# Latent attention's probabilities: transposed by VectorE in 32 by 32 blocks instead of by TensorE

## The chip, the cores and the metric

One core of one Trainium2 chip. The metric is the device time of one execution in microseconds (us). The kernel before has a median of 2431.6 us over 3 runs (2429.13 to 2432.31).

## The reference

Two layers of a hybrid transformer run over one sequence of 256 tokens, width 2048, all in float32. Layer 0 mixes gated linear attention (8 heads) with latent attention (8 heads, 128 columns each plus 64 rotary columns), layer 1 is sparse attention with a compressed, a selected and a window branch; each layer has a gated FFN (5632) and a gated input of 256 columns per token. The part that matters here is the latent attention of layer 0:

```python
q_rope = apply_rope(q[..., MLA_NOPE:], cos64[:, None], sin64[:, None])
k_rope = apply_rope(k_r, cos64, sin64)[:, None]
...
o_mla = causal_attention_blocks(qm, km, kv[..., MLA_NOPE:], (MLA_NOPE + MLA_ROPE) ** -0.5)
...
s = jnp.einsum('bhqd,bhkd->bhqk', qb, k).astype(jnp.float32) * scale
s = jnp.where(kpos[None, :] <= qpos[:, None], s, NEG)
p = jax.nn.softmax(s, axis=-1)
return jnp.einsum('bhqk,bhkd->bhqd', p.astype(v.dtype), v)
```

With 256 tokens and blocks of 128, one head has three 128 by 128 tiles of probabilities: queries 0 to 127 against keys 0 to 127, and queries 128 to 255 against both halves of the keys. The product with the values needs each tile with the keys on the partitions, that is transposed.

## The kernel before, in words

**Weights.** Every weight matrix is streamed from HBM in "units" of 128 partitions by 4 chunks by 512 columns into `raw` (4 buffers, SP's queue, `unit` at L385). To keep float32 accuracy with fp32r products, ScalarE rounds a unit to `wh` (L1048, `split`), VectorE forms the rest `wl = raw - wh` (L1472, `split`), and TensorE multiplies (activations high by `wh`, activations low by `wh`, activations high by `wl`: 24 matmuls of 512 columns, L546). `whl` has two buffers, so ScalarE can round unit n only when the products of unit n-2 are done. TensorE asks for `hi_ready` at a unit's start and for `lo_ready` ahead of its last third.

**Slots and gaps.** Units are grouped in slots; slot s, unit j is written (s, j). Other work is put by hand in the gaps behind units. TensorE does the work of gap (s, j) right behind the products of unit (s, j) (`gap`, L784). ScalarE and VectorE do theirs (`at_gap`, L1187 and L1817) behind the `split` of a later unit, by the tables `STAGED_ACT` and `STAGED_DVE` (L138): two units later in the slots of this change. Each engine works strictly in the order of its program.

**Latent attention** sits in the gaps of slots KG, VG and VG+1 (11, 12, 13; the code writes them as UKV+2 to UKV+4). It takes two heads at a time: `MLA_AT` (L78) puts step t at gaps (11,1), (11,3), (12,1), (12,3), (13,1), (13,3) for t = 0 to 5. On TensorE `mla_step(t)` (L603) first waits for `att_v`, VectorE's word that its stage t-1 is over. Then, for t from 2, it multiplies the values with the transposed probabilities of step t-2 (12 matmuls, L614) from `PT0` into `MB`; for t from 1 to 4 it transposes the six 128 by 128 tiles of step t-1 (L620) from `SP0` through `MB`; for t below 4 it forms the scores of step t (L627 and L633) and signals `s_done`. On VectorE `mla_stage(t)` (L1592) is `softmax` (L1568: scaling and mask from `MB` to `SP0`, two maxima, a wait for ScalarE's exponentials at L1094, a reciprocal, four scalings in place) and, for t from 2, the low part of the output (L1599). Its last instruction signals `att_v`. On ScalarE `mla_stage(t)` (L1097) copies the transposed tiles from `MB` to `PT0` (L1100, one instruction of 128 by 768, signals `pt_sb`), does the exponentials, and rounds the output (L1106). `SP0` and `PT0` have one buffer each. `pt_sb` and `pt_done` are also counted on by the sparse attention of layer 1, behind the 4 steps of latent attention.

The FFN already transposes its hidden activations in another way: `quadrant` (L2029) issues four `V.transpose` instructions (L2036), each on 32 partitions by 256 elements, that transpose 32 by 32 blocks and put them in the right quadrant of partitions of `HT`.

Of the kernel before, what the change touches and what calls it, by code (L numbers as in the profile page):

```python
# [12 lines left out]
ACT = mybir.ActivationFunctionType  # L13
AX = mybir.AxisListType

P = 128
# [10 lines left out]
MLA_SCALE = float((128 + 64) ** -0.5)  # L27
# [48 lines left out]
MLA_STEPS = 4  # L76
NSA_STEPS = 16
MLA_AT = {(UKV + 2, 1): 0, (UKV + 2, 3): 1, (UKV + 3, 1): 2, (UKV + 3, 3): 3, (UKV + 4, 1): 4, (UKV + 4, 3): 5}  # L78


def nsa_plan():
# [114 lines left out]
def build(nc, T):  # L196
# [15 lines left out]
    with ctx:  # L212
# [9 lines left out]
        def sem(name):  # L222
            return ctx.enter_context(nc.semaphore(name))
# [11 lines left out]
        ident = sb("ident", [P, P])  # L235
# [30 lines left out]
        def zt(name, off, shape, dt=F32):  # L266
            assert off + int(np.prod(shape[1:])) * 4 <= ZS, name
            return nc.alloc_sbuf_tensor_at(name, shape, dt, offset=z0 + off)
# [5 lines left out]

        qg, kg = zt("qg", 0, [P, NT, 512]), zt("kg", 4096, [P, NT, 512])
        vg, gg = zt("vg", 8192, [P, NT, 1024]), zt("gg", 16384, [P, NT, 1024])
        SP0, PT0 = zt("SP0", 16384, [P, 2, 384]), zt("PT0", 19456, [P, 2, 384])
        QnT, KnT = zt("QnT", 24576, [P, 8, SEQ]), zt("KnT", 32768, [P, 8, SEQ])
        Vm, zc = zt("Vm", 40960, [P, NT, 1024]), zt("zc", 40960, [P, NT, 1104])
        qr, QrT = zt("qr", 49792, [P, NT, 512]), zt("QrT", 53888, [P, 4, SEQ])  # L280
# [55 lines left out]
        s_done, pt_done, pv_done = sem("s_done"), sem("pt_done"), sem("pv_done")  # L336
        s_read = sem("s_read")
        mx_ok, exp_ok, o_hi = sem("mx_ok"), sem("exp_ok"), sem("o_hi")
        pt_sb = sem("pt_sb")
        att_v, p_ok, head_ok = sem("att_v"), sem("p_ok"), sem("head_ok")  # L340

        ga_ps, ga_t, ga_n, ga_l, ga_ok = (sem(n) for n in ("ga_ps", "ga_t", "ga_n", "ga_l", "ga_ok"))
# [172 lines left out]
        def _(pe):  # L515
# [87 lines left out]
            def mla_step(t):  # L603
                if t:
                    pe.wait_ge(att_v, t)
                if t > 1:
                    pe.wait_ge(pt_sb, min(t - 1, MLA_STEPS))
                if 2 <= t:
                    for b in range(2):
                        hd = 2 * (t - 2) + b  # L610
                        for m in range(NT):
                            for kt in range(m + 1):
                                p0 = (m + kt) * P
                                last = mm(MB[:, 2 * b + m, 384:512], Vm[:, kt, hd * P:(hd + 1) * P],  # L614
                                          PT0[:, b, p0:p0 + P], start=(kt == 0), stop=(kt == m))
                    last.then_inc(pv_done, 1)
                if 1 <= t <= MLA_STEPS:
                    for b in range(2):
                        for k in range(3):
                            last = nc.tensor.transpose(MB[:, 2 + b, k * P:(k + 1) * P],  # L620
                                                       SP0[:, b, k * P:(k + 1) * P], ident[:, :])
                    last.then_inc(pt_done, 1)
                if t < MLA_STEPS:
                    for b in range(2):
                        hd = 2 * t + b
                        for m in range(NT):
                            mm(MB[:, b, m * P:m * P + (m + 1) * P], QnT[:, hd, m * P:(m + 1) * P],  # L627
                               KnT[:, hd, 0:(m + 1) * P], start=(m == 0), stop=False, skip_group_check=True)

                    for m in range(NT):  # L630
                        for b in range(2):
                            r = slice(64 * b, 64 * b + 64)
                            last = mm(MB[:, b, m * P:m * P + (m + 1) * P], QrT[r, t, m * P:(m + 1) * P],  # L633
                                      KrT[r, 0:(m + 1) * P], start=False, stop=True, skip_group_check=True)
                    last.then_inc(s_done, 1)
# [4 lines left out]
            def nsa_step(t):  # L640
                if t == 0:
                    pe.wait_ge(kt_sb, 4)
                if 2 <= t:
                    g, j = (t - 2) // 4, (t - 2) % 4
                    pe.wait_ge(pt_sb, MLA_STEPS + t - 1)
                    pe.wait_ge(pct_sb, g + 1)
                    mm(MB[:, 2, 0:SEQ], VB[:, g, j, :], PcT[:, g % 2, :], start=True, stop=False)  # L647
                    for b, v in enumerate((vs, vw)):
                        mm(MB[:, 2, 0:SEQ], v[:, 0, g * P:(g + 1) * P], PT1[:, b, 0:SEQ], start=False, stop=False)  # L649
                    for b, v in enumerate((vs, vw)):  # L650
                        last = mm(MB[:, 2, P:SEQ], v[:, 1, g * P:(g + 1) * P], PT1[:, b, SEQ:3 * P],  # L651
                                  start=False, stop=b == 1)
                    last.then_inc(pv_done, 1)
                if t in CP_STEP:
                    pe.wait_ge(cs_ok, CP_STEP[t] + 1)
                    for m in range(NT):
                        last = nc.tensor.transpose(MB[:, 3, m * P:(m + 1) * P],
                                                   Pc[:, m, :, :].rearrange("p j n -> p (j n)"), ident[:, :])
                    last.then_inc(cp_ps, 1)
                if t < NSA_STEPS:  # L660
                    g, j = t // 4, t % 4
                    if t:
                        pe.wait_ge(mx_ok, MLA_STEPS + t)
                    else:
                        pe.wait_ge(c2_v, 1)
                        pe.wait_ge(c2_a, 1)
                    for b in range(2):
                        for m in range(NT):
                            last = mm(MB[:, b, m * P:m * P + (m + 1) * P], QT[:, g % 2, j, m * P:(m + 1) * P],  # L669
                                      (ksT, kwT)[b][:, g, 0:(m + 1) * P], start=True, stop=True)  # L670
                    last.then_inc(s_done, 1)
                if 1 <= t <= NSA_STEPS:
                    pe.wait_ge(p_ok, t)
                    if t > 1:
                        pe.wait_ge(head_ok, t - 1)
                    pe.wait_ge(pct_sb, sum(c <= t for c in CP_STEP))
                    for b in range(2):
                        for k in range(3):
                            last = nc.tensor.transpose(MB[:, 2 + b, k * P:(k + 1) * P],  # L679
                                                       SP1[(t - 1) % 2][:, b, k * P:(k + 1) * P], ident[:, :])  # L680
                    last.then_inc(pt_done, 1)
# [351 lines left out]
        def _(act):  # L1033
# [61 lines left out]
                last.then_inc(exp_ok, 1)  # L1095

            def mla_stage(t):  # L1097
                if 1 <= t <= MLA_STEPS:
                    act.wait_ge(pt_done, t)
                    A(PT0[:, :, :], MB[:, 2:4, 0:384], ACT.Copy).then_inc(pt_sb, 1)  # L1100
                if t < MLA_STEPS:
                    exps(t, SP0)
                if t >= 2:
                    act.wait_ge(pv_done, t - 1)
                    for b in range(2):
                        last = A(XBh[:, 2 * (t - 2) + b, :].rearrange("p (m t) -> p m t", m=2),  # L1106
                                 MB[:, 2 * b:2 * b + 2, 384:512], ACT.Copy)
                    last.then_inc(o_hi, 1)

            def nsa_stage(t):  # L1110
                if t >= 2:
                    act.wait_ge(pv_done, MLA_STEPS + t - 1)
                    A(XMID[1][0][:, t - 2, :], MB[:, 2, 0:SEQ], ACT.Copy).then_inc(o_hi, 1)  # L1113
                if t in CP_STEP:
                    g = CP_STEP[t]
                    act.wait_ge(cp_ps, g + 1)
                    A(PcT[:, g % 2, :], MB[:, 3, 0:SEQ], ACT.Copy).then_inc(pct_sb, 1)
                if t < NSA_STEPS:
                    exps(MLA_STEPS + t, SP1[t % 2])
                if 1 <= t <= NSA_STEPS:  # L1120
                    act.wait_ge(pt_done, MLA_STEPS + t)
                    A(PT1[:, :, :], MB[:, 2:4, 0:384], ACT.Copy).then_inc(pt_sb, 1)

            def gla_stage(k):
# [333 lines left out]
        def _(v):  # L1458
# [109 lines left out]
            def softmax(t, SP, scale, gate=None, meanwhile=lambda: None):  # L1568
# [20 lines left out]
                        last = V.tensor_scalar(c, c, sm[:, k:k + 1], None, ALU.mult)  # L1589
                return last  # L1590

            def mla_stage(t):  # L1592
                if t < MLA_STEPS:
                    last = softmax(t, SP0, MLA_SCALE)
                if t >= 2:
                    v.wait_ge(o_hi, t - 1)
                    for b in range(2):
                        x = [q[:, 2 * (t - 2) + b, :].rearrange("p (m t) -> p m t", m=2) for q in XB]
                        last = V.tensor_tensor(x[1], MB[:, 2 * b:2 * b + 2, 384:512], x[0].bitcast(F32), ALU.subtract)  # L1599
                last.then_inc(att_v, 1)  # L1600
# [216 lines left out]
            def at_gap(k):  # L1817
# [2 lines left out]
                    split_in(XB, 4, TQ["cqkv"], 0, 64)  # L1820
                if k in MLA_AT:
                    mla_stage(MLA_AT[k])
                if k in GLA_AT:
                    gla_stage(GLA_AT[k])
                if k == (OUT0, 2):
# [382 lines left out]
```

## Time and profile before

| | |
|---|---|
| median of 3 runs | 2431.6 us |
| profiled execution, own time | 2429.38 us |
| its span in the trace | 2427.7 us |
| granted TensorE clock, mean | 0.999 |
| latent attention's steps on TensorE | from 145 us to 217 us of the span |

The span is the time from the first to the last instruction on the core; the execution's own time is 1.7 us longer. In the views, PE is TensorE's matmuls, PEld its weight loads, DVE VectorE, ACT ScalarE, SP the queue that issues the weights' transfers. A row of the timeline gives the start, the time from there to the end of the last instruction of the row, the engine, the source line, what is written and read, the count, and in brackets the idle time ahead of it on its engine with what ended it.

### The profile page before, as it was taken

What the parts mean: (1) busy time and instruction counts of PE and PEld (TensorE: products, weight loads), DVE (VectorE), ACT (ScalarE), POOL (GpSimd) and SP (SyncE); (2) the same over time, 40 slices, a digit from 0 to 9 for tenths busy, and PEclk for the clock granted to TensorE, in tenths of its full rate; (3) what the DMA queues carried; (4) which work ended last, traced back from release to release, by engine and by line L of the source; (5) the groups of instructions that cost most, each with busy time, mean ns of one, the idle gap of its engine ahead of it and who ended that gap; (6) DMA issues with size and microseconds to landing.
All of it is one profiled execution on the core that took longest, in us unless ns stands there. A gap on an engine that the chain in (4) does not pass through costs nothing.

```text
span 2427.7 us, 29112 instructions
## 1 busy us (share of the span) xinstructions
PE 2398.8 (99%) x11640; PEld 2003.2 (83%) x11640; DVE 1499.5 (62%) x1572; ACT 1047.4 (43%) x1003; POOL 20.5 (1%) x38
## 2 busy tenths in 40 slices
PE   7999999999999999999999999999999999999999
PEld 7887888888888888888888888888888888888887
DVE  4654756666466655667676677566664667446675
ACT  5444445343333433345544355463343434334443
POOL 0000100000000000000000000000000000000000
PEclk9999999999999999999999999999999999999999
DMA  7554456665556556556555633465556665565564
GB/s 227 189 173 125 174 175 211 195 195 194 191 191 191 194 197 196 174 181 219 190 191 179 209 120 107 144 208 191 191 193 196 197 192 190 191 193 193 176 218 138
DMA packets 226967, 449.04 MB, mean 185 GB/s; under 512 B 7961, under 2 KB 19233, under 8 KB 225586
## 3 DMA queue, kind: packets, MB, share of 16 engines
q1 hardware_dynamic: 225218, 440.72, 55.5%
q10 hardware_dynamic: 1648, 6.89, 0.8%
q8 instruction: 74, 1.21, 0.2%
q14 instruction: 27, 0.22, 0.0%
HBM read 445.48 MB, written 2.10 MB: 184 GB/s over the span
## 4 chain that ended last, share of the span: by engine, by line
PE 97%; DVE 2%; ACT 1%; issue 0%; DMA 0%; ACTq 0%; DVEq 0%
PE PG L546 89%; PE MB L546 1%; PE MB L877 1%; PE MB L669 1%; PE MB L649 1%; PE MB L679 0%; ACT whl L1048 0%; DVE whl L1472 0%; PE MB L647 0%; PE MB L651 0%; PE MB L688 0%; PE PG L590 0%; PE PG L591 0%; PE PG L592 0%; PE MB L614 0%
## 5 line engine op out<-in xcount | busy, mean ns | idle before, releaser
L1472 DVE TENSOR_TENSOR whl<-raw,whl 128x2048 fp32r<-128x2048 f32 (+4 forms) x435 | 955.8, 2198 | 762.5 <-ACT whl L1048 762.2
L1048 ACT ACTIVATE whl<-raw 128x2048 fp32r<-128x2048 f32 (+4 forms) x435 | 800.8, 1841 | 1167.0 <-PE PG L546 1151.1
L546 PE MATMUL PG<-whl,XBh 128*128 128x512 f32 (+1 forms) x3376 | 796.6, 386 | 0.9 <-DVE whl L1472 0.5
L546 PE MATMUL PG<-whl,XAh 128*128 128x512 f32 (+1 forms) x3136 | 741.9, 387 | 2.2 <-ACT whl L1048 2.2
L546 PEld LDWEIGHTS PG<-whl,XBh 128*128 128x128 f32 x3376 | 624.9, 188 | 127.5 <-DVE whl L1472 0.9
L546 PEld LDWEIGHTS PG<-whl,XAh 128*128 128x128 f32 x3136 | 584.1, 188 | 119.1 <-ACT whl L1048 3.0
L546 PE MATMUL PG<-whl,XBl 128*128 128x512 f32 (+1 forms) x1688 | 412.5, 386 | 0.0
L546 PE MATMUL PG<-whl,XAl 128*128 128x512 f32 (+1 forms) x1568 | 383.4, 386 | 0.0
L546 PEld LDWEIGHTS PG<-whl,XBl 128*128 128x128 f32 x1688 | 313.1, 188 | 63.2
L546 PEld LDWEIGHTS PG<-whl,XAl 128*128 128x128 f32 x1568 | 291.9, 188 | 57.1
L2036 DVE STREAM_TRANSPOSE HT<-Hb 32x256 f32<-32x256 f32 x352 | 153.4, 436 | 5.6
L1989 DVE TENSOR_TENSOR Hb<-Eb,PG 128x1024 f32<-128x1024 f32 x22 | 26.8, 1216 | 8.8 <-PE PG L546 8.8
L1337 ACT ACTIVATE Eb<-PG,rsh 128x512 f32<-128x512 f32 x44 | 27.5, 675 | 5.4 <-DVE rsq L1522 5.4
L1606 DVE TENSOR_TENSOR XAl<-MB,XAh 128x256 fp32r<-128x256 f32 x16 | 6.8, 423 | 36.3 <-ACT XAh L1113 36.3
L1982 DVE SCALAR_TENSOR_TENSOR Eb<-Eb,PG 128x1024 f32<-128x1024 f32 x22 | 26.7, 1215 | 3.0 <-ACT Eb L1337 3.0
L877 PE MATMUL MB<-ident,h 128*128 128x128 f32 x192 | 26.5, 281 | 0.4 <-ACT posT L1262 0.4
L877 PEld LDWEIGHTS MB<-ident,h 128*128 128x128 f32 x192 | 23.3, 145 | 3.9 <-ACT posT L1262 0.6
L1094 ACT ACTIVATE SP1a<-SP1a,sm 128x128 f32<-128x128 f32 (+1 forms) x32 | 14.2, 445 | 25.0 <-DVE sm L1578 25.0
L503 POOL TENSOR_TENSOR pwo<-pwi,mhalf 128x2 f32<-128x2 f32 (+2 forms) x6 | 8.7, 1445 | 1875.6 <-DVE pwi L1532 1817.2
L1543 DVE SCALAR_TENSOR_TENSOR h<-Fm,pwo,h 128x512 f32<-128x512 f32 (+1 forms) x40 | 23.2, 639 | 0.1
L1094 ACT ACTIVATE SP1b<-SP1b,sm 128x128 f32<-128x128 f32 (+1 forms) x32 | 14.2, 446 | 21.0 <-DVE sm L1578 21.0
L1487 DVE SCALAR_TENSOR_TENSOR XAl<-MB,vcol,XAh 128x256 fp32r<-128x256 f32 x32 | 13.2, 476 | 14.2 <-ACT XAh L1060 14.2
(341 smaller groups left out, 1007.0 us busy)
## 6 DMA issues: line engine op xcount, KB each, us to landing
raw<-in_ffn_w_gate SPq DMA_DIRECT2D x88, 1024.0 KB, 5.2
raw<-in_ffn_w_up SPq DMA_DIRECT2D x88, 1024.0 KB, 5.2
raw<-in_ffn_w_down SPq DMA_DIRECT2D x64, 1024.0 KB, 5.0
raw<-in_nsa_w_in SPq DMA_DIRECT2D x36, 1024.0 KB, 5.1
raw<-in_ple_w_gate SPq DMA_DIRECT2D x32, 1024.0 KB, 5.1
raw<-in_ab_w_in SPq DMA_DIRECT2D x24, 1024.0 KB, 5.3
raw<-in_ffn_w_down SPq DMA_DIRECT2D x32, 768.0 KB, 4.3
raw<-in_ab_w_out SPq DMA_DIRECT2D x16, 1024.0 KB, 5.3
```

The lines of the kernel that those rows point to most:

```text
L546: return mm(bank(m), X[x][:, chunk, m * P:(m + 1) * P], w[:, k, c * ncol:(c + 1) * ncol], start=x == 0 and w is wh and c == 0 and pos in ( ...
L649: mm(MB[:, 2, 0:SEQ], v[:, 0, g * P:(g + 1) * P], PT1[:, b, 0:SEQ], start=False, stop=False)
L669: last = mm(MB[:, b, m * P:m * P + (m + 1) * P], QT[:, g % 2, j, m * P:(m + 1) * P], (ksT, kwT)[b][:, g, 0:(m + 1) * P], start=True, stop= ...
L877: t = nc.tensor.transpose(MB[:, b % 4, o:o + P], h[:, m, k:k + P], ident[:, :])
L1048: A(wh[:, place % 2, 0:w], raw[:, place, 0:w], ACT.Copy).then_inc(hi_ready, 1)
L1094: last = A(c, c, ACT.Exp, bias=sm[:, k:k + 1], accum_out=sm[:, 4 + k:5 + k])
L1337: last = A(Eb[:, m, :], PG[:, b % 2, m, :], ACT.Tanh, scale=rsh[:, 1 + 2 * layer, m:m + 1])
L1472: V.tensor_tensor(wl[:, k, 0:w], raw[:, place, 0:w], wh[:, k, 0:w].bitcast(F32), ALU.subtract).then_inc(lo_ready, 1)
L1543: V.scalar_tensor_tensor(h[:, m, c], Fm[:, m, c], pwo[:, m:m + 1], h[:, m, c], ALU.mult, ALU.add).then_inc(upd, 1)
L1982: V.scalar_tensor_tensor(Eb[:, :, :], Eb[:, :, :], 1.0, PG[:, b % 2, :, :], ALU.add, ALU.mult).then_inc(evac_v, 1)
L1989: V.tensor_tensor(Hb[:, :, :], Eb[:, :, :], PG[:, (b + 1) % 2, :, :], ALU.mult).then_inc(evac_v, 1)
L2036: last = V.transpose(dst[:, :, :, a, :], src[:, :, :, q, :])
```

## The change: what it does

Six transposes on TensorE and the copy on ScalarE are gone from each of the four steps. In their place VectorE issues 16 `V.transpose` instructions for each step, of 32 partitions by 192 elements (2 heads, 3 tiles, 32 columns), from `SP0` to `PT0`. Eight of them (query rows 0 to 63) stand in `mla_stage(t)` behind the softmax, ahead of the signal `att_v`; the other eight (rows 64 to 127) stand in the gap one unit on (`MLT_AT`: (11,2), (12,0), (12,2), (13,0)) and end in the new signal `pt_v`. `PT0` has two buffers, by t % 2; the second lies at byte 50816 of the shared region, behind `KrT`. TensorE's products with the values wait for `pt_v` instead of `pt_sb`, and the next softmax waits for it too, as it writes over `SP0`. The counts of `pt_sb` and `pt_done` in layer 1 lose the 4 steps.

```diff
+MLT_AT = {(UKV + 2, 2): 0, (UKV + 3, 0): 1, (UKV + 3, 2): 2, (UKV + 4, 0): 3}
...
-        SP0, PT0 = zt("SP0", 16384, [P, 2, 384]), zt("PT0", 19456, [P, 2, 384])
+        SP0 = zt("SP0", 16384, [P, 2, 384])
+        PT0 = [zt("PT0a", 19456, [P, 2, 384]), zt("PT0b", 50816, [P, 2, 384])]
...
-        pt_sb = sem("pt_sb")
+        pt_sb, pt_v = sem("pt_sb"), sem("pt_v")
...
             def mla_step(t):
                 if t:
                     pe.wait_ge(att_v, t)
-                if t > 1:
-                    pe.wait_ge(pt_sb, min(t - 1, MLA_STEPS))
                 if 2 <= t:
+                    pe.wait_ge(pt_v, t - 1)
                     for b in range(2):
                         hd = 2 * (t - 2) + b
                         for m in range(NT):
                             for kt in range(m + 1):
                                 p0 = (m + kt) * P
                                 last = mm(MB[:, 2 * b + m, 384:512], Vm[:, kt, hd * P:(hd + 1) * P],
-                                          PT0[:, b, p0:p0 + P], start=(kt == 0), stop=(kt == m))
+                                          PT0[t % 2][:, b, p0:p0 + P], start=(kt == 0), stop=(kt == m))
                     last.then_inc(pv_done, 1)
-                if 1 <= t <= MLA_STEPS:
-                    for b in range(2):
-                        for k in range(3):
-                            last = nc.tensor.transpose(MB[:, 2 + b, k * P:(k + 1) * P],
-                                                       SP0[:, b, k * P:(k + 1) * P], ident[:, :])
-                    last.then_inc(pt_done, 1)
...
             def mla_stage(t):
-                if 1 <= t <= MLA_STEPS:
-                    act.wait_ge(pt_done, t)
-                    A(PT0[:, :, :], MB[:, 2:4, 0:384], ACT.Copy).then_inc(pt_sb, 1)
...
+            def blocks(t, rows):
+                for a in rows:
+                    src = SP0[32 * a:32 * a + 32, :, :].rearrange("p b (k q i) -> p b k q i", k=3, q=4)
+                    for q in range(4):
+                        dst = PT0[t % 2][32 * q:32 * q + 32, :, :].rearrange("p b (k a j) -> p b k a j", k=3, a=4)
+                        last = V.transpose(dst[:, :, :, a, :], src[:, :, :, q, :])
+                return last
+
             def mla_stage(t):   
                 if t < MLA_STEPS:
-                    last = softmax(t, SP0, MLA_SCALE)
+                    if t:
+                        v.wait_ge(pt_v, t)
+                    step(softmax(t, SP0, MLA_SCALE))
+                    last = blocks(t, (0, 1))
                 if t >= 2:
                     v.wait_ge(o_hi, t - 1)
...
                 if k in MLA_AT:
                     mla_stage(MLA_AT[k])
+                if k in MLT_AT:
+                    blocks(MLT_AT[k], (2, 3)).then_inc(pt_v, 1)
```

## Rows read from the trace of the kernel before

**Rows 1.** The page: busy time by engine, and the chain that ended last.

```profile
PE 2398.8 (99%) x11640; PEld 2003.2 (83%) x11640; DVE 1499.5 (62%) x1572; ACT 1047.4 (43%) x1003; POOL 20.5 (1%) x38
...
PE 97%; DVE 2%; ACT 1%; issue 0%; DMA 0%; ACTq 0%; DVEq 0%
```

**Rows 2.** Timeline of PE (and one row of PEld) over latent attention: start us, us, what.

```profile
158.73 0.82 PE L620 MATMUL MB<-ident,SP 128*128 128x128 f32 x6
159.38 1.48 PE L627 MATMUL MB<-KnT,QnT 128*128 128x128 f32 x8
...
161.64 2.11 PE L546 MATMUL PG<-whl,XAh 128*128 128x512 f32 x8
...
172.43 1.21 PEld L614 LDWEIGHTS MB<-PT,Vm 128*128 128x128 f32 x9
...
172.66 1.50 PE L614 MATMUL MB<-PT,Vm 128*128 128x128 f32 x12
174.00 0.82 PE L620 MATMUL MB<-ident,SP 128*128 128x128 f32 x6
...
203.17 1.50 PE L614 MATMUL MB<-PT,Vm 128*128 128x128 f32 x12
204.51 0.82 PE L620 MATMUL MB<-ident,SP 128*128 128x128 f32 x6
205.08 2.08 PE L546 MATMUL PG<-whl,XAh 128*128 128x512 f32 x8
```

**Rows 3.** Timeline of DVE over the same stretch.

```profile
149.88 1.02 DVE L1573 SCALAR_TENSOR_TENSOR SP<-MB,cmask 128x384 f32<-128x384 f32 x2
...
153.87 0.18 DVE L1581 RECIPROCAL sm<-sm 128x4 f32<-128x4 f32 x1 [1.93 <-ACT SP L1094]
154.09 1.01 DVE L1589 TENSOR_SCALAR SP<-SP,sm 128x128 f32<-128x128 f32 x4
155.68 2.29 DVE L1472 TENSOR_TENSOR whl<-raw,whl 128x2048 fp32r<-128x2048 f32 x1 [0.58 <-ACT whl L1048]
160.93 2.29 DVE L1472 TENSOR_TENSOR whl<-raw,whl 128x2048 fp32r<-128x2048 f32 x1 [2.95 <-ACT whl L1048]
163.14 0.74 DVE L1527 TENSOR_SCALAR kg<-PG,rsd 128x512 f32<-128x512 f32 x1
163.80 1.01 DVE L1573 SCALAR_TENSOR_TENSOR SP<-MB,cmask 128x384 f32<-128x384 f32 x2
...
182.21 0.75 DVE L1599 TENSOR_TENSOR XBl<-MB,XBh 128x256 fp32r<-128x256 f32 x2
```

**Rows 4.** Timeline of ACT over the same stretch.

```profile
161.37 0.80 ACT L1100 ACTIVATE PT<-MB 128x768 f32<-128x768 f32 x1
...
182.73 1.92 ACT L1048 ACTIVATE whl<-raw 128x2048 fp32r<-128x2048 f32 x1 [1.15 <-PE PG L546]
```

**Rows 5.** Timeline of DVE in the FFN, where `quadrant` transposes blocks.

```profile
433.43 1.78 DVE L2036 STREAM_TRANSPOSE HT<-Hb 32x256 f32<-32x256 f32 x4
436.66 2.29 DVE L1472 TENSOR_TENSOR whl<-raw,whl 128x2048 fp32r<-128x2048 f32 x1 [1.45 <-ACT whl L1048]
438.99 1.78 DVE L2036 STREAM_TRANSPOSE HT<-Hb 32x256 f32<-32x256 f32 x4
```

**Rows 6.** Lines L2036, L1577 and L1578 on DVE: durations min/median/max in ns.

```profile
L2036 DVE STREAM_TRANSPOSE HT<-Hb x352: 425/436/444, 433.4 to 2273.5; 32x256 f32<-32x256 f32 x176
...
L1577 DVE TENSOR_REDUCE sm<-SP x4: 420/420/421, 150.9 to 194.0; 128x2 f32<-128x256 f32 x4
...
L1578 DVE TENSOR_REDUCE sm<-SP x4: 673/676/678, 151.3 to 194.4; 128x2 f32<-128x512 f32 x4
```

**Rows 7.** Timeline of PE at the start of the kernel.

```profile
15.00 2.82 PE L546 MATMUL PG<-whl,XAh 128*128 128x368 f32 x8 [2.25 <-ACT whl L1048]
...
20.10 2.84 PE L546 MATMUL PG<-whl,XAh 128*128 128x368 f32 x16
```

**Rows 8.** Stretches at the end of the kernel: us, PE busy, granted clock, DMA.

```profile
2420.00:2422.00 2.00, 1.81 (x8) 1.00 0.00 0
2422.00:2424.00 2.00, 0.00 (x0) 1.00 0.00 0
2424.00:2426.00 2.00, 0.00 (x0) 0.63 0.43 161
```

More of the change, by code:

```diff
@@ L644, in nsa_step @@
                     g, j = (t - 2) // 4, (t - 2) % 4
-                    pe.wait_ge(pt_sb, MLA_STEPS + t - 1)
+                    pe.wait_ge(pt_sb, t - 1)
                     pe.wait_ge(pct_sb, g + 1)
@@ L1120, in nsa_stage @@
                 if 1 <= t <= NSA_STEPS:
-                    act.wait_ge(pt_done, MLA_STEPS + t)
+                    act.wait_ge(pt_done, t)
                     A(PT1[:, :, :], MB[:, 2:4, 0:384], ACT.Copy).then_inc(pt_sb, 1)
```

## The prediction

> **What bounds the kernel now.** I read the page first: TensorE is busy for 99% of the span and holds 97% of the chain that ended last [rows 1]. So time is won only by taking work off TensorE, and lost whenever another engine makes it wait. VectorE is busy for 62% on average, but that average says nothing about the 60 us in which latent attention runs, so I then read the timelines of PE, DVE and ACT there.
>
> TensorE [rows 2]: step 1 runs from 158.73 to 161.64 us, 0.65 us of it the six transposes (158.73 to 159.38) and 2.26 us the scores. The two units up to the next step take 11.02 us (161.64 to 172.66). Step 2 begins with 1.34 us of products with the values (172.66 to 174.00). No row of this stretch has idle time in brackets: TensorE waits for nobody.
>
> VectorE [rows 3]: the softmax of step 0 goes from 149.88 to 155.10 us (154.09 plus 1.01), 5.22 us with the 1.93 us in which it waits for ScalarE's exponentials. Behind it comes the split of the next unit at 155.68 us. The bracket there, and the 2.95 us ahead of the next split, are VectorE's slack: two pauses, 0.58 and 2.95 us in these two units, about 3.5 us for a step.
>
> **What is removed.** Four groups of six transposes. The first takes 0.65 us, the last 0.57 us (204.51 to 205.08) [rows 2], the two between 0.66 us each (the first of them 174.00 to 174.66): 2.54 us off TensorE, 0.10% of the kernel. That is the whole possible gain. ScalarE loses four copies of 0.80 us [rows 4]. They are worth nothing: ScalarE's next split waits for TensorE anyway, by 1.15 us even in the fullest stage [rows 4], and VectorE's softmax waits for exponentials that don't come earlier.
>
> **What is added on VectorE.** 64 transposes of 32 by 192, of which the trace has no example. The nearest are those of the FFN, 32 by 256: 0.436 us each [rows 6], four from first start to last end in 1.78 us [rows 5], so (1.78 - 0.436) / 3 = 0.448 us from start to start. They don't overlap. What do 64 elements less save? Two reductions on the same engine, of 256 and 512 elements, take 0.420 and 0.676 us [rows 6]: 1.0 ns for an element. So I take 0.448 - 0.064 = 0.38 us each. The ends: 0.448 if the price doesn't depend on the length, 0.336 if it is all length (three quarters of it). I am nearer the middle because the reduction's two rows show both a fixed and a linear part. Eight transposes are 3.04 us.
>
> **Where they lie.** VectorE has 3.5 us of slack for a step and gets 2 x 3.04 = 6.1 us. So the question is what the deficit does. I walk through VectorE's order, with these pieces: a split followed by block transposes 2.33 us (436.66 to 438.99) [rows 5]; a split followed by something else 2.21 us (160.93 to 163.14) [rows 3]; the eviction of a slot, in every second stage, 0.66 us (163.14 to 163.80) [rows 3]; softmax 5.22 us; the new wait behind it 0.04 us, as the reciprocal's (153.87 plus 0.18, next start 154.09) [rows 3]; the output's low part 0.75 us from step 2 on [rows 3]. `att_v` comes behind the first eight transposes and the low part:
>
> - att_v 1: 155.10 + 0.04 + 3.04 = 158.18 us. TensorE asks for it at 158.73: just in time.
> - att_v 2: split 2.33, eight transposes 3.04, split 2.21, eviction 0.66, softmax 5.22, wait 0.04, eight transposes 3.04, together 16.54: 174.72 us. TensorE, with step 1 now 2.26 us, is there at 158.73 + 2.26 + 11.02 = 172.01: it waits 2.71 us.
> - att_v 3: the same without the eviction and with 0.75 us of low part, 16.63: 191.35 us. TensorE: 174.72 + 1.34 + 2.26 + 11.02 = 189.34: it waits 2.01 us.
> - att_v 4: 16.63 + 0.66 = 17.29: 208.64 us. TensorE: 191.35 + 14.62 = 205.97: it waits 2.67 us.
> - Steps 4 and 5 have no softmax. att_v 5 comes 2.33 + 3.04 + 2.21 + 0.75 = 8.3 us later, at 217.0; TensorE needs it 1.34 + 11.02 = 12.4 us later. No wait.
>
> Step 4's products end at 208.64 + 1.34 = 209.98 us, where they and the transposes ended at 205.08 [rows 2]. That is **4.9 us lost**, or as a sum, 7.39 us of new waits less 2.54 us of transposes. Nothing gives it back, since TensorE runs without idle time behind it.
>
> What hangs on the other waits. Queued behind `att_v` on TensorE are the products of two units; ScalarE's next splits wait for those, but VectorE reaches them later still: the split of (12,3) needs (12,1), done at 172.0, and VectorE takes it at 174.72 + 2.33 + 3.04 = 180.1. `pt_v` is never late: the first comes at 158.18 + 2.33 + 3.04 = 163.6 us and TensorE asks at 172. The splits themselves come up to 7 us later than now, but TensorE needs the low part of (12,0) only in the last third of that unit, which without transposes starts at 160.99 + 3.6 = 164.6 us, and gets it at 160.5 instead of 157.97 [rows 3]. SP's transfers issue behind the splits, one unit of four each; they slip with them, with a unit's buffer still asked for two units later. No DMA is added.
>
> **The restart.** Without a wait the first weight load runs ahead of its product (172.43 against 172.66) [rows 2]. Behind a wait this 0.23 us is bare. Only the last wait's counts, because VectorE sets the pace of the others: 0.2 us. From below it is nothing.
>
> A long wait could also cost TensorE its clock. The rows show both levels. At the end of the kernel TensorE is idle from about 2421.8 us; the granted clock is still 1.00 up to 2424 and 0.63 in the two microseconds after [rows 8], on the way from 2.4 to 1.2 GHz. And at the start, after little work and 2.25 us of idle time, 8 matmuls of 368 columns took 2.82 us, where later 16 took 2.84 [rows 7]: the pace of 1.2 GHz, at a price of 1.4 us. My waits are 2.0 to 2.7 us, each with over 11 us of full work on both sides, where at the end no work followed and at the start little stood before; so I take nothing and keep 1.4 us for the range. The Trainium skill ("TensorE: Matmul & The Clock Gate", Why this matters for your kernels) warns against idle gaps of this order between bursts of matmuls, as they put the clock back to its lower level. The fall at the end of this trace agrees; whether a gap inside full work does it, no row shows. By that rule the sum would be 5.1 + 1.4 = +6.5 us.
>
> **Sum.** 4.9 + 0.2 = +5.1 us. Durations are from one execution of 2429.38 us (span 2427.7, 1.7 us lie around it), 2.2 us under the median: 2434.5 us for such an execution, and on the median of 2431.6 us **2436.7 us**. A measurement of this kernel can tell about 0.2% from no change, 4.9 us. My forecast stands on that line, so "same" and "slower" are nearly even.
>
> The number that decides is the price of one transpose: 56 of the 64 stand on the path (8 + 3 x 16). At 0.448 us it is 5.1 + 56 x 0.068 = +8.9 us (2440.5), at 0.336 us 5.1 - 56 x 0.044 = +2.6 us (2434.2). The result would be zero at 0.29 us.
>
> **Rivals.**
>
> 1. *The cover holds: not slower.* VectorE's four scalings, of 128 and 256 elements, mean 192, take 1.01 us together, 0.25 us each [rows 3]. If block transposes of this size ran at that pace, att_v 4 would come at 208.64 - 56 x 0.13 = 201.4 us and TensorE, never stopped, would ask at 158.73 + 13.28 + 2 x 14.62 = 201.25. There would be 0.1 us of waits and a gain of 2.4 us: 2429.2 us. The point from which it decides is a price under 0.25 us. Against it: 352 transposes of a third more elements are never under 0.425 us [rows 6]. Chance 0.06.
> 2. *The full price.* 192 elements cost like 256: +8.9 us, 2440.5 us. For it: a transpose of small size might be bound by its fixed part. Against it: the slope of the reductions. Chance 0.10.
> 3. *The clock falls in the last wait.* In the first two waits it would cost nothing, as TensorE stands before the next wait with 2 us in hand; behind the third it is paid, 1.4 us: +6.5 us, 2438.1 us. For it: the lower pace at the start [rows 7]. Against it: full work on both sides of each wait. Chance 0.08. The rule of the Trainium skill named above would give this case.
> 4. *The change doesn't do what it says*: some transposes still on TensorE's path, or `pt_v` the wait that ends last. By the diff and the times above neither can be: 0.01.
>
> The forecast, VectorE the bound for three steps with +2.6 to +7 us, has 0.75.
>
> **The numbers.** The range takes in the whole price range and the clock, and about 1 us on each side for the measurement: 2432.5 to 2441.0 us. It leaves out rival 1 and the far end of rival 2. Within the forecast the line of 4.9 us lies 0.2 us under the middle, just what the restart may not cost: 0.36 slower, 0.39 same. Rival 2 is slower (0.10), rival 3 nearly always (0.07, same 0.01), rivals 1 and 4 are within 0.2% (0.05) but for 0.02, as a gain over 0.2% would need twice what the transposes hold. Slower 0.53, same 0.45, faster 0.02.
>
> **What the changed profile would show.** `V.transpose` at 0.37 to 0.39 us, 64 times. DVE without pauses, other than for the exponentials, from 155 to 208 us. Idle time on PE ahead of the products with the values at three steps, 2 to 3 us each, ended by VectorE's transposes or by the low part; none ahead of step 1 and steps 4 and 5's units. PE busy 2.5 us less. PEclk 1.00 throughout. I am wrong if PE shows no such waits, if a wait in front of an L546 product shows up, or if the clock falls.

## The result, and the profile after

The changed kernel takes 2436.31 us in the median (2435.95 to 2438.59, 9 runs) against 2431.58 us before (2428.97 to 2432.31, 9 runs). The ratio of the means is 1.0025, 95% interval 1.0016 to 1.0034: slower by a quarter of a per cent (the medians alone differ by 4.7 us, 0.19%). The forecast was 2436.7 us.

The page of the changed kernel, its busy times and its chain, against [rows 1]:

```profile
PE 2402.3 (99%) x11616; PEld 2005.3 (82%) x11616; DVE 1523.2 (63%) x1636; ACT 1044.1 (43%) x999; POOL 20.5 (1%) x38
...
PE 94%; DVE 4%; ACT 1%; issue 1%; DMA 0%; ACTq 0%; DVEq 0%
```

TensorE has 24 instructions less and yet 3.5 us *more* busy time, where 2.5 us less was forecast: a first sign that some of its work ran slower. VectorE has 64 instructions and 23.7 us more, its share of the chain rises from 2% to 4%. Which waits are new, the list of PE's waits says (total us, times, longest us); the other lines of the list are those of the kernel before, but for 0.2 us in the very first one:

```profile
PE MB L615 <- DVE PT0b L1591: 2.9, 1, 2.9
...
PE MB L615 <- DVE XBl L1604: 2.6, 2, 2.4
```

L615 is the product with the values, L1591 the block transpose, L1604 the low part of the output, the two instructions that end VectorE's stage. VectorE's timeline over two steps, against [rows 3] (start us, us from there to the last end, and in brackets idle time ahead):

```profile
156.71 1.01 DVE L1581 TENSOR_SCALAR SP<-SP,sm 128x128 f32<-128x128 f32 x4
157.75 3.04 DVE L1591 STREAM_TRANSPOSE PT0a<-SP 32x192 f32<-32x192 f32 x8
160.83 2.29 DVE L1464 TENSOR_TENSOR whl<-raw,whl 128x2048 fp32r<-128x2048 f32 x1
163.16 3.06 DVE L1591 STREAM_TRANSPOSE PT0a<-SP 32x192 f32<-32x192 f32 x8
166.25 2.29 DVE L1464 TENSOR_TENSOR whl<-raw,whl 128x2048 fp32r<-128x2048 f32 x1
168.46 0.75 DVE L1519 TENSOR_SCALAR kg<-PG,rsd 128x512 f32<-128x512 f32 x1
169.12 1.01 DVE L1565 SCALAR_TENSOR_TENSOR SP<-MB,cmask 128x384 f32<-128x384 f32 x2
...
173.12 0.18 DVE L1573 RECIPROCAL sm<-sm 128x4 f32<-128x4 f32 x1 [1.94 <-ACT SP L1089]
...
174.37 3.05 DVE L1591 STREAM_TRANSPOSE PT0b<-SP 32x192 f32<-32x192 f32 x8
```

No bracket but the one for ScalarE's exponentials: VectorE has no slack left. Its first eight transposes end at 157.75 + 3.04 = 160.79 us, the next step's at 177.42: 16.63 us apart, where the sum gave 16.54. TensorE, against [rows 2]:

```profile
161.35 1.48 PE L622 MATMUL MB<-KnT,QnT 128*128 128x128 f32 x8
...
177.68 2.90 PE L615 MATMUL MB<-PT0a,Vm 128*128 128x128 f32 x12 [2.91 <-DVE PT0b L1591]
...
194.18 1.60 PE L615 MATMUL MB<-PT0b,Vm 128*128 128x128 f32 x12 [0.26 <-DVE XBl L1604]
...
211.44 2.93 PE L615 MATMUL MB<-PT0a,Vm 128*128 128x128 f32 x12 [2.38 <-DVE XBl L1604]
...
225.34 1.50 PE L615 MATMUL MB<-PT0b,Vm 128*128 128x128 f32 x12
226.60 2.09 PE L548 MATMUL PG<-whl,XAh 128*128 128x512 f32 x8
```

Step 1 (161.35) doesn't wait, steps 2, 3 and 4 do, step 5 doesn't. Look at the second column: the same 12 matmuls take 1.50 us at step 5 and 2.9 us at steps 2 and 4, behind the two long waits. The stretches of the same trace (start and end, length, PE busy and its instructions, granted clock, DMA share and GB/s) say why:

```profile
176.00:177.00 1.00, 0.00 (x0) 1.00 0.00 0
...
178.00:179.00 1.00, 1.00 (x6) 0.50 0.00 0
...
178.00:182.00 4.00, 4.00 (x22) 0.68 0.28 42
182.00:189.00 7.00, 7.00 (x36) 1.00 0.71 229
...
209.00:212.00 3.00, 0.62 (x3) 0.88 0.00 0
212.00:220.00 8.00, 8.00 (x37) 0.83 0.44 131
```

The clock went from 2.4 to 1.2 GHz towards the end of both long waits and came back some microseconds later: at step 2 it is still 1.00 while TensorE stands idle at 176 us, 0.50 when the products run at 178, and 1.00 again from 182.

**A yardstick.** Whole executions scatter by 2 to 3 us, as much as most effects here. So I measure in each trace the *latent stretch*: from the first score product of step 0 to the first product of weights behind step 5. Before it is 217.32 - 145.47 = 71.85 us, by these rows of the kernel before:

```profile
145.47 1.48 PE L627 MATMUL MB<-KnT,QnT 128*128 128x128 f32 x8
...
217.32 2.08 PE L546 MATMUL PG<-whl,XAh 128*128 128x512 f32 x8
```

In the changed kernel the scores of step 0 start at 148.09, so it is 226.60 - 148.09 = 78.51 us: **+6.66 us**. The start itself lies 2.6 us later in this trace, which is no effect of the change; the section on unexpected hardware shows what it is.

### The profile page after: what moved, and what is told of

Its sections match the earlier page's. It is cut to its first block, busy times and chain, and to the rows that moved or that the text cites. A ratio compares the mean times of both kernels' runs of the same rounds, so it can differ in the third digit from the quotient of the medians.

```text
span 2436.9 us, 29127 instructions
## 1 busy us (share of the span) xinstructions
PE 2402.3 (99%) x11616; PEld 2005.3 (82%) x11616; DVE 1523.2 (63%) x1636; ACT 1044.1 (43%) x999; POOL 20.5 (1%) x38
## 4 chain that ended last, share of the span: by engine, by line
PE 94%; DVE 4%; ACT 1%; issue 1%; DMA 0%; ACTq 0%; DVEq 0%
PE PG L548 87%; PE MB L548 1%; DVE whl L1464 1%; PE MB L872 1%; PE MB L664 1%; PE MB L644 1%; DVE PT0a L1591 0%; ACT whl L1043 0%; PE MB L674 0%; DVE PT0b L1591 0%; PE MB L642 0%; PE MB L646 0%; ACT SP L1089 0%; PE MB L683 0%; PE PG L592 0%
```

## The experiments

All start from the changed kernel.

**1. The removal alone.** Block transposes only in step 0; the products of all steps read its buffer.

```diff
-                    pe.wait_ge(pt_v, t - 1)
+                    pe.wait_ge(pt_v, 1)
...
-                                          PT0[t % 2][:, b, p0:p0 + P], start=(kt == 0), stop=(kt == m))
+                                          PT0[0][:, b, p0:p0 + P], start=(kt == 0), stop=(kt == m))
...
-                    last = blocks(t, (0, 1))
+                    if t == 0:
+                        last = blocks(t, (0, 1))
...
-                if k in MLT_AT:
+                if MLT_AT.get(k) == 0:
```

> Left out: the probabilities of steps 1 to 3 are not transposed at all; their products with the values read the transposed tiles of step 0. Everything else is the changed kernel. Measured on the latent stretch, from the first score product of step 0 to the first product behind step 5 (71.85 us before, 78.51 us changed). Theory (VectorE's time is the cost, the transposes on TensorE held 2.54 us): 71.85 - 2.54 = 69.3 us, no wait on TensorE, clock 1.00, about 2.5 us under the kernel before. Rival (the new signals, buffers or places cost by themselves): clearly above 70 us.

Measured: 2428.57 us, ratio to the kernel before 0.9991 (0.9982 to 1.0001). The rows of PE at both ends of the stretch:

```profile
146.72 1.48 PE L622 MATMUL MB<-KnT,QnT 128*128 128x128 f32 x8
...
214.77 1.50 PE L615 MATMUL MB<-PT0a,Vm 128*128 128x128 f32 x12
216.03 2.08 PE L548 MATMUL PG<-whl,XAh 128*128 128x512 f32 x8
```

216.03 - 146.72 = 69.31 us, no wait in between, clock 1.00. The 24 transposes on TensorE held exactly their 2.54 us. The first step's block transposes, the first buffer and the new signal cost nothing; the second buffer is not used here, but run 7, which uses both, comes out at its sum too. The loss of the change is thus the block transposes of steps 1 to 3 on VectorE, with what they set off: 9.2 us against this run.

**2. The signal early.** `att_v` behind the softmax and the low part, ahead of the first eight block transposes.

```diff
-                    step(softmax(t, SP0, MLA_SCALE))
-                    last = blocks(t, (0, 1))
+                    last = softmax(t, SP0, MLA_SCALE)
                 if t >= 2:
...
                 last.then_inc(att_v, 1)
+                if t < MLA_STEPS:
+                    v.wait_ge(att_v, t + 1)
+                    blocks(t, (0, 1))
```

> att_v is signalled behind the softmax and the output's low part, ahead of the first eight block transposes; the same 64 transposes are done. Theory (VectorE's throughput over three steps is the bound; the eight ahead of att_v count only once): att_v 1 to 4 at 155.1, 171.7, 188.3, 205.6 us in the time of the kernel before, against TensorE at 158.7, 172.0, 186.6, 202.9: waits of 0, 0, 1.7 and 2.7 us, latent stretch 73.9 us, or 75.4 us if the clock falls in the last wait. Rival (what costs is that TensorE waits for transposes behind the softmax, nothing else): no waits, 69.3 us.

Measured: 2434.14 us, ratio 1.0013 (1.0003 to 1.0022). PE:

```profile
148.12 1.48 PE L622 MATMUL MB<-KnT,QnT 128*128 128x128 f32 x8
...
174.63 1.55 PE L615 MATMUL MB<-PT0a,Vm 128*128 128x128 f32 x12
...
190.99 1.60 PE L615 MATMUL MB<-PT0b,Vm 128*128 128x128 f32 x12 [1.54 <-DVE XBl L1603]
...
208.25 2.93 PE L615 MATMUL MB<-PT0a,Vm 128*128 128x128 f32 x12 [2.37 <-DVE XBl L1603]
...
223.43 2.09 PE L548 MATMUL PG<-whl,XAh 128*128 128x512 f32 x8
```

The stretch is 75.31 us, forecast 75.4 with the clock's fall. Waits of 0, 1.54 and 2.37 us: the wait at step 2 is gone, those at 3 and 4 stay. So the place of the signal was worth 3.2 us once (78.51 less 75.31), and behind it stands VectorE's throughput, which moving the signal did not change. The fall is seen behind the last wait alone (2.93 us for the 12 matmuls), not behind the wait of 1.54 us.

**3. All sixteen behind the softmax.** The same 64 transposes, none of them one unit on.

```diff
-                    last = blocks(t, (0, 1))
+                    last = blocks(t, (0, 1, 2, 3))
+                    last.then_inc(pt_v, 1)
+                    v.wait_ge(pt_v, t + 1)
...
-                if k in MLT_AT:
-                    blocks(MLT_AT[k], (2, 3)).then_inc(pt_v, 1)
...
-                last.then_inc(att_v, 1)
+                if t in (0, 1):
+                    v.sem_inc(att_v, 1)
+                else:
+                    last.then_inc(att_v, 1)
```

> All sixteen block transposes of a step stand behind its softmax and ahead of att_v, none one unit on. Theory (throughput): only the first step's eight more are new on the path, 8 x 0.38 = 3.0 us: a wait at step 1 too, latent stretch about 81.4 us. Rival (only transposes ahead of att_v cost, those one unit on are free): the three waits grow by 3 us each, latent stretch about 87 us or more.

Measured in a single execution: 2439.36 us, span 2437.7 us. PE:

```profile
145.91 1.48 PE L622 MATMUL MB<-KnT,QnT 128*128 128x128 f32 x8
...
161.80 2.39 PE L622 MATMUL MB<-KnT,QnT 128*128 128x128 f32 x8 [2.47 <-DVEq L1608]
...
227.45 2.09 PE L548 MATMUL PG<-whl,XAh 128*128 128x512 f32 x8
```

81.54 us: 3.0 us more than the changed kernel, once, with a new wait at step 1; not 3 us at each wait. The transposes one unit on are as much on the path as those ahead of the signal. VectorE's whole work between two signals counts. The waits at steps 1 to 4 are 2.47, 1.67, 1.62 and 2.22 us. The clock fell at the first (2.39 us for 8 matmuls that take 1.48) and the last, not at the two between.

**4 to 6. Is the clock's fall paid?** TensorE gets products of zeros to do ahead of its wait, in the accumulators that it already holds.

```diff
             def mla_step(t):
+                if 2 <= t <= MLA_STEPS:
+                    if t == 3:
+                        banks_free(VG + 1)
+                    for k in range(18):
+                        mm(PG[:, (VG if t == 2 else VG + 1) % 2, k % 2, 0:P], cmask[:, 1, :], cmask[:, 1, :],
+                           start=t == 3, stop=t == 3, skip_group_check=True)
                 if t:
```

> The changed kernel with 18 products of zeros by zeros (128 by 128 by 128, 2.0 us) ahead of TensorE's wait for att_v in steps 2, 3 and 4, so that TensorE works where it idled. Theory (the clock falls in the waits of steps 2 and 4, and the fall behind the last one is paid): the clock stays at 1.00, the latent stretch falls by 1.5 us to 77.0 us, though TensorE has 54 products more. Rival (the clock's fall costs nothing, VectorE sets the end): 78.5 us or more.

This one missed: 2439.28 us, ratio 1.0037 (1.0023 to 1.0051). A float32 product is two matmuls here, so that the filling was twice as long as meant and longer than the waits:

```profile
171.98 4.18 PE L610 MATMUL PG<-cmask 128*128 128x128 f32 x36
```

The stretch was 81.34 us at clock 1.00 throughout; it says nothing of the question but that an overfull wait is paid in full: the 69.31 us of run 1 and three times 4.01 us from the first filling product to the next work (171.98 to 175.99) make 81.34. With `range(8)`:

> As the run before with 18 products, but 8 of them in each of the three waits: each float32 product turned out to be two matmuls of 0.11 us, so 18 were 4.0 us and more than the waits; 8 are 1.8 us, less than each wait. Theory (the clock's fall behind the last wait is paid): clock 1.00 in the whole stretch, VectorE sets the three waits as before, latent stretch 77.0 us against the 78.5 us of the changed kernel, though TensorE does 48 matmuls more. Rival (the fall costs nothing): 78.5 us.

The profile gave what the theory asks, clock 1.00 and a stretch of 225.10 - 148.11 = 76.99 us:

```profile
177.49 1.60 PE L621 MATMUL MB<-PT0a,Vm 128*128 128x128 f32 x12 [0.92 <-DVE PT0b L1597]
```

The times did not: 2437.95 us in the median (2434.65 to 2438.75, 8 runs), ratio 1.0027 (1.0016 to 1.0038), above the changed kernel's, though the lowest was 1.3 us under it. In six of these eight executions 2.5 to 3.1 us lie outside the span, where all the others of this study have 1.7 to 1.8; why stays open. Counted by spans the median is 2435.2 us, against 2434.6 for the changed kernel, still not lower. Inconclusive. So once more with less idle rest, `range(8 if t == 3 else 11)`, and the changed kernel itself was timed again:

> As the run with 8 products in each wait, with 11, 8 and 11 (2.5, 1.8 and 2.5 us by 0.224 us each), so that under 0.4 us of each wait is left idle. The run with 8 showed clock 1.00 and a latent stretch of 76.99 us in its profile, but its times do not show the 1.5 us. Theory (the clock's fall is a matter of TensorE idling, and the idle rests of up to 0.9 us still let it fall in some executions): latent stretch 77.0 us in the profile, and in the times of all executions a lowest about 1.4 us under the lowest of the changed kernel and nearly none above 2437.3 us. Rival (filling the waits does nothing for the clock, the one profile was luck): times like those of the changed kernel, 2436.0 to 2438.6 us.

> The changed kernel unaltered, on the same chip and in the same rounds as the run with the closely filled waits. Theory: latent stretch 78.5 us again, waits of 2.7 to 2.9 us at step 2 and about 2.4 us at step 4 with the clock under 1.00 behind both, times from 2436.0 to 2438.6 us. Rival (the falls in the first profile were chance): a stretch of 77.0 us with clock 1.00 and waits of 2.7, 2.0 and 2.7 us.

The two were not timed together, as the second of these expectations has it: they ran on different chips at different times, each beside its own runs of the kernel before. The clock is the mean granted clock of each whole execution.

| | latent stretch | median | lowest to highest | clock |
|---|---|---|---|---|
| changed kernel again | 78.56 us | 2436.66 us | 2435.58 to 2438.88, 9 runs | 0.997 to 0.999 |
| waits filled closely | 76.95 us | 2435.91 us | 2434.78 to 2437.68, 11 runs | 0.999 to 1.000 |

Ratios to the kernel before: 1.0025 (1.0015 to 1.0035) and 1.0023 (1.0014 to 1.0032); the two overlap, so by the times of whole executions the difference is not shown. The lowest is 0.8 us under the changed kernel's instead of 1.4, and one execution of 11 is above 2437.3 us, where the changed kernel has three of 9. The clocks of the executions do differ, and in the traces the time does too. The changed kernel again, the stretches behind its waits of 2.90 and 2.37 us:

```profile
175.00:178.00 3.00, 2.94 (x15) 0.57 0.00 0
...
210.00:214.00 4.00, 4.00 (x16) 0.63 0.43 91
```

and the same stretches with filled waits:

```profile
175.00:178.00 3.00, 2.76 (x23) 1.00 0.00 0
...
210.00:214.00 4.00, 4.00 (x25) 1.00 0.20 26
```

The rows of PE with filled waits show where the time is saved:

```profile
146.65 1.48 PE L628 MATMUL MB<-KnT,QnT 128*128 128x128 f32 x8
...
209.99 1.60 PE L621 MATMUL MB<-PT0a,Vm 128*128 128x128 f32 x12
...
223.60 2.09 PE L548 MATMUL PG<-whl,XAh 128*128 128x512 f32 x8
```

From the first scores to the products behind the last wait both take the same, 209.99 - 146.65 = 63.34 us here and 211.44 - 148.09 = 63.35 us in the changed kernel, so the first fall costs nothing. From there to the end of the stretch it is 13.61 against 15.16 us: the last fall is paid, 1.55 us. Two traces of the changed kernel have 78.5 us, two with filled waits 77.0 us, with up to 60 matmuls more. What is left, 76.95 - 71.85 = 5.10 us, is VectorE's pace alone.

**7. A version that fits the slack.** `att_v` early as in 2, and step 1's tiles back on TensorE and ScalarE; VectorE transposes steps 0, 2 and 3.

```diff
+ON_PE = (1,)
...
+                    if t - 2 in ON_PE:
+                        pe.wait_ge(pt_sb, ON_PE.index(t - 2) + 1)
+                    else:
+                        pe.wait_ge(pt_v, on_v(t - 2))
...
+                if t - 1 in ON_PE:
+                    for b in range(2):
+                        for k in range(3):
+                            last = nc.tensor.transpose(MB[:, 2 + b, k * P:(k + 1) * P],
+                                                       SP0[:, b, k * P:(k + 1) * P], ident[:, :])
+                    last.then_inc(pt_done, 1)
...
+                if t - 1 in ON_PE:
+                    act.wait_ge(pt_done, ON_PE.index(t - 1) + 1)
+                    A(PT0[(t - 1) % 2][:, :, :], MB[:, 2:4, 0:384], ACT.Copy).then_inc(pt_sb, 1)
...
-                if k in MLT_AT:
+                if k in MLT_AT and MLT_AT[k] not in ON_PE:
```

> att_v early as in the run with the early signal, and step 1's six tiles transposed by TensorE and copied by ScalarE as in the kernel before; VectorE transposes those of steps 0, 2 and 3. Theory (VectorE's slack carries one step's 6.1 us at a time, not two in a row): att_v 2, 3, 4 at about 171.7, 182.3 and 199.6 us in the time of the kernel before, TensorE there at 172.0, 187.3 and 201.9: no wait, clock 1.00, latent stretch 71.85 - 0.65 - 0.66 - 0.57 = 69.97 us, 1.9 us or 0.08% under the kernel before. Rival (any block transposes in the stretch make TensorE wait): above 71.85 us.

Measured: 2428.94 us, ratio 0.9992 (0.9983 to 1.0001). PE and, below it, DVE in the same trace:

```profile
147.71 1.48 PE L636 MATMUL MB<-KnT,QnT 128*128 128x128 f32 x8
...
189.57 1.50 PE L623 MATMUL MB<-PT0b,Vm 128*128 128x128 f32 x12
...
204.17 1.50 PE L623 MATMUL MB<-PT0a,Vm 128*128 128x128 f32 x12
...
217.68 2.09 PE L553 MATMUL PG<-whl,XAh 128*128 128x512 f32 x8
```

```profile
174.52 4.49 DVE L1481 TENSOR_TENSOR whl<-raw,whl 128x2048 fp32r<-128x2048 f32 x2 [0.58 <-ACT whl L1057]
...
201.32 0.74 DVE L1620 TENSOR_TENSOR XBl<-MB,XBh 128x256 fp32r<-128x256 f32 x2
```

217.68 - 147.71 = 69.97 us, the number that was forecast, without a wait. In the step left to TensorE VectorE even idles again (0.58 us), and its signal for step 4 comes at 202.06 us, where TensorE asks at 204.17. This version is 1.9 us faster than the kernel before by its trace; by whole executions the interval still takes in 1, so the gain is not shown there. Against run 2 (75.31 us), which has the signal early too, keeping step 1 off VectorE is worth 5.3 us; whether three steps would fit with the signal where the change has it was not tried.

## Why the prediction was right, and where it was lucky

- *The price of a transpose.* Forecast 0.38 us from start to start, from the two reductions of [rows 6]. The group in the trace of the changed kernel, 370 ns of one, eight in 3.04 to 3.06 us:

```profile
L1591 DVE STREAM_TRANSPOSE PT0a<-SP 32x192 f32<-32x192 f32 x32 | 11.8, 370 | 0.5
```

- *VectorE as the bound of three steps.* Right to 0.1 us for each piece: 16.63 us between the first two signals against 16.54, no wait at steps 1 and 5. With the clock held up, the loss is 5.10 us, the forecast +5.1 us.
- *The restart.* Forecast 0.2 us at the last wait, from the bare weight load. From the end of VectorE's last instruction to TensorE's first product there are 0.26 us at step 2 (177.42 to 177.68), but only 0.05 at step 4 (211.39 to 211.44), the wait that counts. In its place the pieces between the first and the fourth signal came out 0.14 us longer than their sum (50.60 against 50.46). That +5.1 us is met so exactly is thus partly chance.
- *The removal's value.* 2.54 us forecast, 2.54 us measured (run 1).
- *The cover of ScalarE's copies, the splits and the transfers.* Nothing new waits for them; right.
- *The clock.* Here a step failed: "so I take nothing and keep 1.4 us for the range". Two of the signs named in advance failed with it: PE busy, 3.5 us more instead of 2.5 less, and the clock, 1.00 throughout by the forecast. It fell in both long waits, in both traces of the changed kernel. Rival 3, given 0.08, is what happens, in the manner described there: the first fall costs nothing since VectorE sets the pace (TensorE's slower work eats the next wait: 0.26 us where 2.01 were forecast), the last one is paid, 1.55 us against 1.4 forecast. The whole loss in the stretch is 6.66 us; rival 3 gave 6.5. My reason against it, full work on both sides of the wait, doesn't protect. The sentence of the Trainium skill that was set against it ("TensorE: Matmul & The Clock Gate", Why this matters for your kernels) pointed to the better number. But it warns of gaps somewhat longer than any wait here, so it reaches this case only if taken loosely, which the prediction did without saying so; the traces agree that an idle gap puts the clock back, and show it for waits of 2.2 to 2.9 us inside full work.
- *The median* then hit within 0.4 us by luck, for a reason that I hadn't in mind: executions of either kernel fall into two groups over 2 us apart, and the shorter kind was more frequent in the changed kernel's first nine runs (7 of 9) than in those of the kernel before (4 of 9). Group against group, the means of the shorter executions differ by 6.9 us (2436.25 and 2429.34), those of the longer by 6.5 us (2438.37 and 2431.86): the 6.7 us of the traces, not the 4.7 us between the medians.

## What to carry to other kernels

Before work is moved to an engine with a low average load, add up that engine's order of work between two signals of the stretch concerned: 62% over the kernel was 3.5 us of slack for a step here, and 6.1 us were put on it to save 0.65. Where the slack is too small, move only so much as it holds; with the signal early, three of four steps gave 1.9 us in the trace and all four cost 3.5; as changed, all four cost 6.7. And where a wait opens on TensorE, add the clock's fall to its price if no later wait absorbs it: here all seven waits of 2.2 to 2.9 us in latent attention had it (two in each trace of the changed kernel, one in run 2, two in run 3), and the three of 1.5 to 1.7 us there had not.

## What was not expected of the hardware

**The clock falls in short waits, and at one of them not in every execution.** The kernel before has a wait of 1.54 us at 86 us of the span, ahead of a transpose. In its trace the unit behind it starts with 8 matmuls in 2.09 us:

```profile
87.44 2.09 PE L546 MATMUL PG<-whl,XAh 128*128 128x512 f32 x8
```

In the trace of the changed kernel, behind the same wait of 1.54 us:

```profile
88.51 3.61 PE L548 MATMUL PG<-whl,XAh 128*128 128x512 f32 x8
```

with a granted clock of 0.92 and 0.91 in the two stretches of 10 us around it. The fall showed in 4 of the 10 traces of this study (the changed kernel's first and those of runs 2, 5 and 7), and costs 1.6 us: from this wait's end to the first scores of latent attention it is about 61.0 us with it and 59.4 without. Another 1.0 us lies at the start. 0.2 us of it is the very first wait, 0.8 us the work from 17.6 us on, before and then changed:

```profile
17.62 1.29 PE L877 MATMUL MB<-ident,h 128*128 128x128 f32 x8
...
17.81 1.91 PE L872 MATMUL MB<-ident,h 128*128 128x128 f32 x8
```

That this is how soon the clock rises is inferred from the pace; the granted clock reads 1.00 there in both traces. Together they are the 2.6 us by which the changed kernel's first profile started the latent stretch later. Its second trace has neither: its stretch starts at 145.48 us, and its execution took 2435.97 us, 2.6 us less than the 2438.59 of the first. They also fit the two groups in the times of the kernel before (2429 and 2432 us), of which only one of the shorter kind was traced. Why it falls in one execution and not in the next at the same wait no run here shows.

**Block transposes don't overlap each other.** 0.370 us of duration and 0.382 us from start to start, where the four scalings of the softmax, 0.28 to 0.35 us long, take 1.01 us together and so do overlap. A split ahead of them is not overlapped either (2.33 us instead of 2.21), as [rows 5] had shown.
